# The v rows of an expert layer: every row gathered whole, against half of each row gathered and the other half multiplied from streamed tiles

## The chip, the cores and the metric

One NeuronCore of one Trainium2 chip runs the whole program in one launch. The metric is the device time of an execution in microseconds (us). The core has five engines: TensorE (PE; its weight loads are PEld), VectorE (DVE), ScalarE (ACT), GpSimd (POOL) and SyncE (SP), and 16 DMA engines that all queues share.

## The reference

Two transformer blocks on 256 tokens of width 2048, in fp32. The change touches only the last layer of the second block. For each token, 8 heads choose 16 experts each out of 128 x 128, so 128 experts a token. An expert is a row of `peer_u` and a row of `peer_v`, 2048 floats (8 KB) each.

```python
top_s, top_i = lax.top_k(s, PEER_TOPK)          # per head, two lists of 128 keys
cand_i = (top_i[:, :, 0, :, None] * N_KEYS + top_i[:, :, 1, None, :])...
best_s, best_j = lax.top_k(cand_s, PEER_TOPK)
idx = jnp.take_along_axis(cand_i, best_j, axis=-1)
g = jax.nn.softmax(best_s, axis=-1)
u_sel = jnp.take(u, idx, axis=0)
a = jax.nn.gelu(jnp.einsum('thkd,td->thk', u_sel, hb), approximate=False)
v_sel = jnp.take(v, idx, axis=0)
return jnp.einsum('thk,thkd->td', (g * a).astype(hb.dtype), v_sel)
```

## The kernel before, in words

The 256 tokens are two token tiles of 128, one token to a partition. Everything ahead of the expert layer is a list of products whose weights SyncE streams in tiles of 512 KB; the last of them, `query`, gives the scores. `read_scores(c)` on ScalarE hands the scores of two heads over, and `choose(t, c)` on VectorE turns them into 32 expert numbers a token (t is the token tile, c the pair of heads), so 8 calls in all. The first two calls stand ahead of the first dot product.

The expert layer works in slots. Slot (row) j of token tile t is one gather: an indirect DMA from GpSimd's queue fetches for each of the 128 tokens the row of its j-th expert, 128 rows of 8 KB, 1.05 MB, into one of 16 buffers `rows_buf`. There are 256 such slots for u and 256 for v. The order is by half tile (`hx`, 64 slots): 64 gathers of u, 64 of v, and so on. GpSimd issues in that order, and a gather waits until its pair of buffers has been used (`rows_used`).

- u slots: VectorE multiplies the row by `hb` and adds up (`dot_products`), 2048 columns.
- `coefs(hx)`: gelu of the 64 dots on ScalarE, times the softmax gate, gives a coefficient per token and slot.
- v slots: half of them VectorE adds to `h` with `scalar_tensor_tensor` (`weigh_rows`), the other half TensorE adds up in PSUM: ScalarE makes a diagonal matrix of the coefficients (`diag`), TensorE multiplies it by the row, four products of 512 columns. `add_sums` adds the four banks of a token tile to `h`.
- The calls choose(0, 2) to choose(1, 3) stand between the weighings, two in each of the first three v phases. SyncE writes the output in 8 pieces when the sums are there.

What starts when is set by the order in each engine's own instruction stream and by counting semaphores. An engine that waits holds everything behind it in its stream. For GpSimd that is every later gather.

## Time and profile before

| | |
|---|---|
| Three runs | 3399.82, 3405.42, 3406.12 us; median 3405.42 |
| Profiled execution, span from first to last instruction | 3402.5 us (its time apart from the span is not given) |
| DMA share and rate, 2134 to 3385 us | 1.01, 426 GB/s |
| Data of the indirect gathers (queue q0) | 536.97 MB of 868.10 MB |
| Instructions | 42238 |

The span is cut into stretches by the view of windows, which gives for each the busy time of each engine with its number of instructions, the clock granted to TensorE as a share of the higher level, the busy share of the 16 DMA engines and their GB/s. The expert layer is the stretch from the first dot product at 2134 us to the end. An engine's idle time matters only where the others wait for it.

### The profile page before, as it was taken

Reading aid. Unit: us, or ns where it says so; the run is one execution under the profiler, and the core shown is the slowest. Engines: PE = TensorE matmul, PEld = TensorE weight load, DVE = VectorE, ACT = ScalarE, POOL = GpSimd, SP = SyncE. Lnnn points to the kernel's source line nnn. Section 1 sums busy time; section 2 is a strip of 40 time slices with the busy share of each in tenths; the row PEclk is TensorE's granted clock in tenths of the full one; section 3 lists DMA queues with packets and bytes.
Section 4 is the critical chain, followed back from the end, with each engine's and each line's share of the span. In section 5 each row is a group of like instructions: output and inputs, shape, how many; then the busy total and the mean of one; then the engine's idle time right before and its main releaser. Section 6 shows DMA issues by size and latency. Waiting matters only on the chain.

```text
span 3402.5 us, 42238 instructions
## 1 busy us (share of the span) xinstructions
PE 2507.2 (74%) x15833; PEld 1974.7 (58%) x15833; DVE 1781.8 (52%) x2456; ACT 1081.7 (32%) x2108; POOL 2364.1 (69%) x1677
## 2 busy tenths in 40 slices
PE   7999996989999999989999899108503730571077
PEld 5777885779988998889988679103201310230032
DVE  4375656242200223220412446997797879778954
ACT  6444424464444444454546554000000100000000
POOL 7400316859999999987866579886687578568853
PEclk9999997999999999999999999559856965796589
DMA  5684300546655665555544346999999999999998
GB/s 180 206 237 145 105 3 26 185 123 183 185 191 187 183 183 185 187 153 161 161 131 125 117 164 206 396 427 427 427 428 427 427 427 427 428 426 427 427 427 344
DMA packets 241376, 868.10 MB, mean 255 GB/s; under 512 B 18940, under 2 KB 21484, under 8 KB 174886
## 3 DMA queue, kind: packets, MB, share of 16 engines
q0 software_dynamic: 73776, 536.97, 37.5%
q1 hardware_dynamic: 163414, 316.11, 30.6%
q10 hardware_dynamic: 4016, 12.75, 1.3%
q8 instruction: 106, 1.74, 0.2%
q14 instruction: 64, 0.52, 0.0%
HBM read 860.24 MB, written 2.10 MB: 253 GB/s over the span
## 4 chain that ended last, share of the span: by engine, by line
PE 50%; POOL 19%; DMA 11%; DVE 7%; issue 4%; ACT 1%; DVEq 0%; ACTq 0%; POOLq 0%; SPq 0%
PE acc L2022 20%; PE acc L2032 19%; DMA zone<-in_peer_v,zone 10%; POOL lasting L736 10%; POOL zone L736 9%; PE acc L2028 3%; PE acc L2160 3%; PE acc L2586 2%; POOL w_lo L616 1%; DVE lasting L1962 1%; DMA lasting<-in_peer_u,zone 1%; PE acc L2475 1%; DVE zone L1568 0%; PE acc L2069 0%; DVE x_lo L1697 0%
## 5 line engine op out<-in xcount | busy, mean ns | idle before, releaser
L616 POOL TENSOR_TENSOR w_lo<-lasting,w_hi 128x512 fp32r<-128x512 f32 x1024 | 1372.4, 1359 | 276.0 <-ACT w_hi L785 257.3
L785 ACT ACTIVATE w_hi<-lasting 128x512 fp32r<-128x512 f32 (+1 forms) x1184 | 741.3, 631 | 903.6 <-PE acc L2022 457.0
L2586 PE MATMUL acc<-zone,lasting 128*128 128x512 f32 x512 | 256.3, 655 | 694.3 <-ACT lasting L1297 643.4
L2586 PEld LDWEIGHTS acc<-zone,lasting 128*128 128x128 f32 x512 | 105.2, 210 | 841.6 <-ACT lasting L1297 505.2
L2032 PE MATMUL acc<-x_hi,w_hi 128*128 128x256 f32 (+1 forms) x1856 | 305.5, 286 | 11.5 <-DVE x_lo L1697 4.3
L736 POOL DMA_INDIRECT zone<-in_peer_v,zone x128 | 192.2, 1502 | 165.6 <-DVE lasting L1962 73.6
L1932 DVE CUSTOM_DVE_ANT_0 zone<-zone 128x2048 f32<-128x2048 f32 x128 | 293.4, 2292 | 21.9 <-DMA zone<-in_peer_u,zone 7.1
L1932 DVE CUSTOM_DVE_ANT_0 zone<-lasting,zone 128x2048 f32<-128x2048 f32 x128 | 293.5, 2293 | 21.0 <-DMA lasting<-in_peer_u,zone 8.6
L2032 PE MATMUL acc<-x_lo,w_hi 128*128 128x256 f32 (+1 forms) x1856 | 298.6, 283 | 0.0
L2032 PE MATMUL acc<-x_hi,w_lo 128*128 128x256 f32 (+1 forms) x1856 | 298.3, 283 | 0.0
L2586 PE MATMUL acc<-lasting 128*128 128x512 f32 x512 | 247.8, 635 | 64.9 <-DMA zone<-in_peer_v,zone 38.2
L736 POOL DMA_INDIRECT lasting<-in_peer_u,zone x128 | 248.5, 1942 | 58.4 <-issue 36.9
L736 POOL DMA_INDIRECT zone<-in_peer_u,zone x128 | 256.7, 2005 | 42.7 <-issue 37.8
L2032 PEld LDWEIGHTS acc<-x_hi,w_hi 128*128 128x128 f32 x1856 | 255.0, 189 | 19.1 <-issue 7.7
L2032 PEld LDWEIGHTS acc<-x_lo,w_hi 128*128 128x128 f32 x1856 | 255.3, 189 | 0.0
L2032 PEld LDWEIGHTS acc<-x_hi,w_lo 128*128 128x128 f32 x1856 | 254.4, 189 | 0.0
L736 POOL DMA_INDIRECT lasting<-in_peer_v,zone x128 | 199.5, 1558 | 72.7 <-issue 35.6
L1289 ACT ACTIVATE zone<-zone 128x64 f32<-128x64 f32 x4 | 1.0, 256 | 744.7 <-DVEq L1936 744.7
L2022 PE MATMUL acc<-w_hi,x_hi 128*128 128x512 f32 (+1 forms) x672 | 216.0, 403 | 19.5 <-DVE w_lo L1379 8.8
L2586 PEld LDWEIGHTS acc<-lasting 128*128 128x128 f32 x512 | 101.3, 203 | 209.4 <-issue 196.3
L2022 PE MATMUL acc<-w_hi,x_lo 128*128 128x512 f32 (+1 forms) x672 | 211.1, 396 | 0.0
L2022 PE MATMUL acc<-w_lo,x_hi 128*128 128x512 f32 (+1 forms) x672 | 209.6, 393 | 0.0
(419 smaller groups left out, 3951.7 us busy)
## 6 DMA issues: line engine op xcount, KB each, us to landing
lasting<-in_w_in SPq DMA_DIRECT2D x200, 512.0 KB, 3.7
lasting<-in_w_up SPq DMA_DIRECT2D x128, 512.0 KB, 3.8
lasting<-in_w_down SPq DMA_DIRECT2D x128, 512.0 KB, 3.6
lasting<-in_w_mix_out SPq DMA_DIRECT2D x32, 512.0 KB, 3.6
lasting<-in_w_out SPq DMA_DIRECT2D x32, 512.0 KB, 3.6
lasting<-in_peer_w_query SPq DMA_DIRECT2D x32, 512.0 KB, 3.7
lasting<-in_w_kv_cross SPq DMA_DIRECT2D x16, 512.0 KB, 3.7
lasting<-in_w_q_cross SPq DMA_DIRECT2D x8, 512.0 KB, 3.7
```

What stands on the lines that cost most here:

```text
L616: pool.tensor_tensor(w_lo[:, k, 0:width], ring[:, slot, s % SLOT_SLABS, 0:width], w_hi[:, k, 0:width].bitcast(FP32), ALU.subtract).then_in ...
L736: pool.indirect_dma_start(out=rows_buf[2 * n + k], out_offset=None, in_=A[table][0], in_offset=bass.IndirectOffsetOnAxis(ap=experts[:, hx ...
L785: act.activation(w_hi[:, s % PARTS, 0:width], ring[:, slot, s % SLOT_SLABS, 0:width], ACT.Copy).then_inc(hi_ready, 1)
L1289: act.activation(part, part, ACT.Gelu).then_inc(s_gelu, 1)
L1932: last = dve.tensor_tensor_reduce(out=junk, in0=rows_buf[2 * n + k], in1=hb[:, t], scale=1.0, scalar=0.0, op0=ALU.mult, op1=ALU.add, accum ...
L1962: last = STT(h[:, t], rows_buf[2 * n + k], coef[:, t, slot:slot + 1], h[:, t], ALU.mult, ALU.add)
L2022: last = pe.matmul(bank(banks[t])[:, 0:width], xp[:, s, g.lo + t * P:g.lo + (t + 1) * P], wp[:, k, 0:width], **kw)
L2028: last = pe.matmul(bank(banks[f // 2])[:, f % 2 * SEQ:(f % 2 + 1) * SEQ], wp[:, k, f * P:(f + 1) * P], xp[:, s, g.lo:g.hi], skip_group_che ...
L2032: last = pe.matmul(bank(banks[f])[:, 0:g.hi - g.lo], wp[:, k, f * P:(f + 1) * P], xp[:, s, g.lo:g.hi], **kw)
L2160: return pe.matmul(out, lhsT, rhs, start=start, stop=stop, skip_group_check=check)
L2475: last = pe.matmul(two_out(m), probT2[0:size, m % 2, n * P:(n + 1) * P], v, start=n == 0, stop=n == t + 1)
L2586: last = pe.matmul(bank(4 * t + c), diag[:, n // 2, k], rows_buf[2 * n + k][:, c * CHUNK:(c + 1) * CHUNK], start=hx % 2 == 0 and i == 0 an ...
```

## The change

The v part is split by columns. Columns 1024 to 2047 are still gathered, one slot at a time, as half rows of 4 KB (0.52 MB a gather, `gather_v`). Columns 0 to 1023 are computed without a gather: the coefficients of a token tile are spread into a matrix of 16384 experts by 128 tokens (`dense0`, `dense1`), and the left half of the whole table `peer_v` is streamed by SyncE in tiles of 128 experts by 1024 columns (0.52 MB) and multiplied by it on TensorE (`v_product`).

The matrix is built from one-hot vectors: for each token, TensorE multiplies the one-hots of its 128 slots by the second key with those by the first key, the latter scaled by the coefficients (`dense_group`, four tokens a group, 32 groups a token tile). ScalarE builds the one-hots of the first token tile (`one_hots` by Abs and Relu), VectorE those of the second (by `is_equal`); ScalarE copies the products out of PSUM (`read_dense`).

The order: all 256 u slots first (`gather_u`), with 16 buffers for the first token tile and 7 for the second. From u slot 80 on a v half row follows each u slot until 72 have been sent (`V_AFTER`, `V_EARLY`); TensorE adds these up by diagonals, all of the first token tile. 48 diagonals come ahead of the first matrix, 24 are interleaved with its groups. The other 184 half rows are weighed by VectorE, with 6 buffers. Calls of `choose` come behind u slots 2, 92, 132, 160 and 192, coefficients behind 66, 129, 220 and 255; three calls of choose stand ahead of the first dot. No tile is streamed until all dots are done. Then 11 tiles are multiplied for the first token tile alone while the second matrix is built; these 11 are loaded again for the second token tile, and the other 117 are used for both: 139 loads, 5 places. `choose` also writes the numbers of the half rows and `split_experts` the two keys of each slot.

The core of the diff:

```diff
+        FIRST_TILE, SECOND_TILE = (5, 7, 8, 13, 4, 6, 0, 1, 9, 10, 11, 12, 14, 15), (5, 7, 8, 13, 4, 16, 18)
+        U_BUF = [q if q < 16 else FIRST_TILE[(q - 16) % 14] if q < P else SECOND_TILE[(q - P) % 7] for q in range(U_SLOTS)]
+        U_SEM = [b if b < 16 else b - 7 for b in U_BUF]
+        U_USE = [U_SEM[:q].count(U_SEM[q]) for q in range(U_SLOTS)]
+        U_BEFORE = [max([k for k in range(q) if U_SEM[k] == U_SEM[q]], default=None) for q in range(U_SLOTS)]
+        V_EARLY = 72
+        V_AFTER = {80 + k: k for k in range(V_EARLY)}
+        CHOICES = [(t, c) for t in range(TILES) for c in range(4)]
+        CHOSEN = {choice: n + 1 for n, choice in enumerate(CHOICES)}
+        CHOOSE_AFTER = dict(zip((2, 92, 132, 160, 192), CHOICES[3:]))
+        COEFS_AFTER = {66: 0, 129: 1, 220: 2, 255: 3}
...
+        LATE_HALVES = half_rows + [at(3 * D, HALF_D), at(7 * HALF_D, HALF_D)]
+        half_of_slot = lambda q: half_rows[q % 4] if q < V_EARLY else LATE_HALVES[(q - V_EARLY) % 6]
+        ALONE_BEFORE, ALONE_BESIDE = 0, 11
+        ALONE = ALONE_BEFORE + ALONE_BESIDE
+        V_LOADS = [(i, (0,)) for i in range(ALONE)] + [(i, (1,)) for i in range(ALONE)] + [(i, (0, 1)) for i in range(ALONE, N_KEYS)]
...
+            for n, (i, tiles) in enumerate(V_LOADS):
+                if n == 0:
+                    sp.wait_ge(s_wpe, V_EARLY)
+                if n == ALONE_BEFORE:
+                    sp.wait_ge(s_dot, 2 * TILES)
+                elif n >= ALONE_BEFORE + len(V_SPOTS):
+                    sp.wait_ge(slab_used, v_used(n - len(V_SPOTS)))
+                if n >= 4:
+                    sp.wait_ge(*v_landed(n - 4))
+                sp.dma_start(v_tile(n), A["peer_v_2"][0][i * P:(i + 1) * P, 0:HALF_D]).then_inc(v_landed(n)[0], 16)
...
+            def gather_u(q):
+                t, j, b = q // P, q % P, U_BUF[q]
+                if j % 32 == 0:
+                    pool.wait_ge(s_ix0, CHOSEN[t, j // 32])
+                if U_USE[q]:
+                    pool.wait_ge(s_dotted, U_BEFORE[q] + 1)
+                if b == 16:
+                    pool.wait_ge(s_ix0, CHOSEN[0, 3])
+                elif b == 18:
+                    pool.wait_ge(s_dot, 2)
                 pool.indirect_dma_start(
...
+            def gather_v(q):
+                t, j = q // P, q % P
+                if q >= V_EARLY + 6:
+                    pool.wait_ge(s_wdve, q - 6 - V_EARLY + 1)
+                elif q >= V_EARLY + 4:
+                    pool.wait_ge(s_dot, 2 * TILES)
+                elif q >= V_EARLY:
+                    pool.wait_ge(slab_used, v_used(ALONE_BEFORE - 4 + q - V_EARLY))
+                elif q >= 4:
+                    pool.wait_ge(s_wpe, q - 4 + 1)
+                else:
+                    pool.wait_ge(s_dotted, 4)
+                pool.indirect_dma_start(
+                    out=half_of_slot(q), out_offset=None, in_=v_halves,
+                    in_offset=bass.IndirectOffsetOnAxis(ap=half_rows_no[:, t, j:j + 1], axis=0)
+                ).then_inc(half_landed(q)[0], 16)
...
+            for q in range(7, U_SLOTS):
+                if q == 13:
+                    pool.wait_ge(s_sp, 4)
+                gather_u(q)
+                if q in V_AFTER:
+                    gather_v(V_AFTER[q])
+            for q in range(V_EARLY, U_SLOTS):
+                gather_v(q)
...
+            def diagonal(q):
+                if q >= 4:
+                    act.wait_ge(s_wpe, q - 4 + 1)
+                act.activation(diag[:, q % 4], ident, ACT.Copy, scale=coef[:, 0, q:q + 1]).then_inc(s_diag, 1)
+            def one_hots(g):
+                if g >= 2:
+                    act.wait_ge(s_dense, g - 1)
+                for n in range(4):
+                    s_ = 4 * g + n
+                    for k in range(2):
+                        last = act.activation(hot_of(g, k)[:, n], key_no, ACT.Abs, scale=-1.0, bias=keysT[:, k, s_:s_ + 1])
+                step(last)
+                step(act.activation(one_hot[:, g % 2], one_hot[:, g % 2], ACT.Relu, scale=-1.0, bias=1.0))
+                for n in range(4):
+                    s_ = 4 * g + n
+                    last = act.activation(hot_of(g, 1)[:, n], hot_of(g, 1)[:, n], ACT.Copy, scale=coefT[:, 0, s_:s_ + 1])
+                last.then_inc(s_hot, 1)
+            def read_dense(g):
+                act.wait_ge(s_dense, g + 1)
+                act.activation(dense[g // 32][:, :, 4 * (g % 32):4 * (g % 32) + 4], bank(6 + g % 2).rearrange("p (n c) -> p c n", n=4), ACT.Copy).then_inc(s_denseR, 1)
...
+            gelu_dots(1)
+            exp_gates(2)
+            act.wait_ge(s_coefs, 2)
+            read_keys(0)
+            read_coefs(0)
+            for g in range(GROUPS // TILES):
+                one_hots(g)
+                if g:
+                    read_dense(g - 1)
+                if 48 + g < V_EARLY:
+                    diagonal(48 + g)
+            read_dense(GROUPS // TILES - 1)
+            exp_gates(3)
+            gelu_dots(2)
+            read_keys(1)
+            gelu_dots(3)
+            read_coefs(1)
+            for g in range(GROUPS // TILES, GROUPS):
+                read_dense(g)
...
+            def dot_product(q):
+                t, j, b = q // P, q % P, U_BUF[q]
+                dve.wait_ge(u_full[U_SEM[q]], 16 * (U_USE[q] + 1))
+                dve.tensor_tensor_reduce(out=junk, in0=u_rows[b], in1=hb[:, t], scale=1.0, scalar=0.0,
+                                         op0=ALU.mult, op1=ALU.add, accum_out=dots[:, t, j:j + 1]).then_inc(s_dotted, 1)
+                dve.drain()
...
+            def one_hots(g):
+                dve.wait_ge(s_dense, g - 1)
+                for n in range(4):
+                    s_ = 4 * (g - GROUPS // TILES) + n
+                    TS(hot_of(g, 0)[:, n], key_no, keysT[:, 2, s_:s_ + 1], None, ALU.is_equal)
+                    last = TS(hot_of(g, 1)[:, n], key_no, keysT[:, 3, s_:s_ + 1], coefT[:, 1, s_:s_ + 1], ALU.is_equal, ALU.mult)
+                last.then_inc(s_hot, 1)
+            def weigh_half_row(q):
+                t, j = q // P, q % P
+                dve.wait_ge(*half_landed(q))
+                STT(h[:, t, HALF_D:], half_of_slot(q), coef[:, t, j:j + 1], h[:, t, HALF_D:], ALU.mult, ALU.add).then_inc(s_wdve, 1)
+                dve.drain()
...
+            for t, c in CHOICES[:3]:
+                dve.wait_ge(s_sc, c + 1)
+                choose(t, c)
+            dve.wait_ge(lo_ready, G["query"].slab(0, 3, SLABS - 1) + 1)
+            for q in range(U_SLOTS):
+                dot_product(q)
+                if q % HALF_ROWS == HALF_ROWS - 1:
+                    dve.nop().then_inc(s_dot, 1)
+                if q in CHOOSE_AFTER:
+                    t, c = CHOOSE_AFTER[q]
+                    if t == 0:
+                        dve.wait_ge(s_sc, c + 1)
+                    choose(t, c)
+                    if c == 3:
+                        split_experts(t)
+                if q in COEFS_AFTER:
+                    coefs(COEFS_AFTER[q])
+            dve.wait_ge(s_keysR, 2)
+            dve.wait_ge(s_coefR, 2)
+            done = V_EARLY
+            for g in range(GROUPS // TILES, GROUPS):
+                one_hots(g)
+                if g % 2:
+                    weigh_half_row(done)
+                    done += 1
+            dve.wait_ge(s_wpe, V_EARLY)
             for c in range(2):
+                add_bank(0, 2 + c, 4 + c)
+                dve.drain()
+            for q in range(done, U_SLOTS):
+                weigh_half_row(q)
+            dve.wait_ge(slab_used, v_used(len(V_LOADS) - 1))
+            for t in range(TILES):
+                for c in range(2):
+                    add_bank(t, c, 2 * t + c)
...
+            def weigh_half_row(q):
+                pe.wait_ge(s_diag, q + 1)
+                pe.wait_ge(v_full[q % 4], 16 * (q // 4 + 1))
+                for c in range(2):
+                    last = pe.matmul(bank(4 + c), diag[:, q % 4], half_rows[q % 4][:, c * CHUNK:(c + 1) * CHUNK],
+                                     start=q == 0, stop=q == V_EARLY - 1)
+                last.then_inc(s_wpe, 1)
...
+            def dense_group(g):
+                pe.wait_ge(s_hot, g + 1)
+                if g >= 2:
+                    pe.wait_ge(s_denseR, g - 1)
+                for n in range(4):
+                    last = pe.matmul(bank(6 + g % 2)[:, n * P:(n + 1) * P], hot_of(g, 1)[:, n], hot_of(g, 0)[:, n], start=True, stop=True)
+                last.then_inc(s_dense, 1)
...
+            def v_product(n):
+                i, tiles = V_LOADS[n]
+                pe.wait_ge(*v_landed(n))
+                for t in tiles:
+                    for c in range(2):
+                        last = pe.matmul(bank(2 * t + c), dense[t][:, i], v_tile(n)[:, c * CHUNK:(c + 1) * CHUNK],
+                                         start=i == 0, stop=i == N_KEYS - 1)
+                last.then_inc(slab_used, 1)
...
+            for g in range(GROUPS // TILES):
+                dense_group(g)
+                if 48 + g < V_EARLY:
+                    weigh_half_row(48 + g)
...
+            turn_keys(1)
+            turn_coefs(1)
+            for g in range(GROUPS // TILES, GROUPS):
+                dense_group(g)
+                if g % 3 == 2 and (g - GROUPS // TILES) // 3 < ALONE_BESIDE:
+                    v_product(ALONE_BEFORE + (g - GROUPS // TILES) // 3)
+            pe.wait_ge(s_denseR, GROUPS)
+            for n in range(ALONE, len(V_LOADS)):
+                v_product(n)
```

## Rows read from the trace of the kernel before

**Rows 1.** Windows: busy us (instructions) by engine, granted clock, DMA share, GB/s

```profile
2134.00:3385.00 1251.00, 492.58 (x1029) 205.10 (x1027) 991.46 (x1026) 57.29 (x149) 890.01 (x506) 0.71 1.01 426
...
2900.00:3000.00 100.00, 63.87 (x128) 26.28 (x128) 74.97 (x99) 8.26 (x26) 56.91 (x35) 0.81 1.01 427
3000.00:3100.00 100.00, 61.23 (x128) 25.39 (x128) 73.92 (x96) 5.48 (x11) 65.77 (x44) 0.87 1.01 427
```

**Rows 2.** Groups by line and shape, 2134 to 3402 us: busy us, mean ns, idle before

```profile
L1932 DVE CUSTOM_DVE_ANT_0 zone<-zone 128x2048 f32<-128x2048 f32 x128 | 293.4, 2292 | 21.9 <-DMA zone<-in_peer_u,zone 7.1 <-DMA lasting<-in_peer_u,zone 4.9
L736 POOL DMA_INDIRECT lasting<-in_peer_u,zone x127 | 247.4, 1948 | 58.2 <-issue 36.9 <-PE acc L2586 21.3
L736 POOL DMA_INDIRECT zone<-in_peer_v,zone x128 | 192.2, 1502 | 165.6 <-DVE lasting L1962 73.6 <-PE acc L2586 57.0 <-issue 33.1
L1962 DVE SCALAR_TENSOR_TENSOR lasting<-zone,lasting 128x2048 f32<-128x2048 f32 x64 | 150.5, 2351 | 104.5 <-DMA zone<-in_peer_v,zone 101.4 <-issue 0.4 <-DVE zone L1921 0.2
```

**Rows 3.** Timeline of GpSimd: start us, us, instruction

```profile
2271.35 2.13 POOL L736 DMA_INDIRECT zone<-in_peer_u,zone  x1 [0.30 <-issue]
...
2317.59 0.95 POOL L736 DMA_INDIRECT lasting<-in_peer_v,zone  x1 [0.30 <-issue]
2318.84 0.95 POOL L736 DMA_INDIRECT lasting<-in_peer_v,zone  x1 [0.30 <-issue]
```

**Rows 4.** Timeline of VectorE: two dots, then one call of choose

```profile
2134.32 2.29 DVE L1932 CUSTOM_DVE_ANT_0 zone<-zone 128x2048 f32<-128x2048 f32 x1
...
2146.42 2.29 DVE L1932 CUSTOM_DVE_ANT_0 zone<-lasting,zone 128x2048 f32<-128x2048 f32 x1
...
2326.30 0.30 DVE L1883 MAX8 zone<-zone 128x8 f32<-128x128 f32 x1
...
2339.41 0.19 DVE L1908 TENSOR_TENSOR zone<-zone 128x32 f32<-128x32 f32 x1
...
2344.49 0.19 DVE L1921 SCALAR_TENSOR_TENSOR zone<-zone 128x32 uint32<-128x32 f32 x1
```

**Rows 5.** DMA issues from 2200 to 2260 us: count, median us to landing

```profile
lasting<-in_peer_u,zone POOLq DMA_INDIRECT x14, 9.6
```

**Rows 6.** Windows: weight tiles of 2 KB rows alone, columns as in rows 1

```profile
175.00:176.80 1.80, 1.80 (x10) 1.46 (x9) 0.69 (x1) 0.06 (x1) 0.00 (x0) 1.00 1.03 363
```

**Rows 7.** ScalarE: timeline of two stretches, then groups by line

```profile
2125.22 1.01 ACT L1276 ACTIVATE zone<-acc 128x1024 f32<-128x1024 f32 x1
...
2290.80 2.45 ACT L1297 ACTIVATE lasting<-lasting,zone 128x128 f32<-128x128 f32 x8 [0.84 <-DVEq L1953]
...
L988 ACT ACTIVATE zone<-acc 128x512 f32<-128x512 f32 x18 | 9.8, 594 | 4.2 <-PE acc L2022 4.2
```

**Rows 8.** TensorE: timeline of eight products, and line 2586's ns min/median/max

```profile
3351.50 3.60 PE L2586 MATMUL acc<-zone,lasting 128*128 128x512 f32 x8
...
L2586 PE MATMUL acc<-lasting x512: 592/592/1193, 2303.9 to 3392.0; 128*128 128x512 f32 x171
```

**Rows 9.** VectorE: timeline of two short operations, then groups by line

```profile
2339.52 0.17 DVE L1912 TENSOR_SCALAR zone<-zone 128x32 uint32<-128x32 uint32 x1
2339.60 0.17 DVE L1913 TENSOR_SCALAR zone<-zone 128x32 uint32<-128x32 uint32 x1
...
L1808 DVE TENSOR_SCALAR zone<-acc,lasting 128x128 f32<-128x128 f32 x16 | 5.6, 351 | 0.6
L1477 DVE TENSOR_TENSOR zone<-zone 128x1024 f32<-128x1024 f32 x2 | 2.4, 1218 | 0.0
```

**Rows 10.** The end: windows as in rows 1, then VectorE's timeline

```profile
3380.00:3385.00 5.00, 4.59 (x11) 1.71 (x9) 2.68 (x2) 0.00 (x0) 0.00 (x0) 1.00 0.62 262
3385.00:3390.00 5.00, 2.77 (x4) 1.31 (x5) 2.02 (x1) 0.00 (x0) 0.00 (x0) 0.76 0.06 26
...
3397.05 2.48 DVE L1973 TENSOR_TENSOR lasting<-acc,lasting 128x512 f32<-128x512 f32 x4 [0.26 <-issue]
```

More of the change, by code:

```diff
@@ L131, in build @@
         with nc.sbuf_tensor("lasting", [P, BASE], FP32) as lasting, nc.sbuf_tensor("zone", [P, TOTAL - BASE], FP32) as zone_all:
+            pass
+        with nc.sbuf_tensor("before_dense", [P, X0 + 1024], FP32), nc.sbuf_tensor("dense0", [P, P * N_KEYS], FP32) as dense0, nc.sbuf_tensor("dense1", [P, P * N_KEYS], FP32) as dense1:
             pass
@@ L378, in build @@
+        v_tile = lambda n: half_rows[n % 4] if n < ALONE_BEFORE else at(V_SPOTS[spot_of(n)], HALF_D)
         G = {}
@@ L404, in build @@
         following = dict(zip(list(G)[:-1], list(G)[1:]))
+        TURNS = sum(g.turns * g.bodies for g in G.values())
         tile_full = [sem(f"tile_full{i}") for i in range(SLOTS)]
@@ L741, in _ @@
-            early = [(0, 0), (0, 1), (1, 0), (1, 1), (2, 0)]
-            rests("query", after={at_: lambda n=n, k=k: gather(0, 0, n, k) for at_, (n, k) in zip(((2, 15), (3, 2), (3, 5), (3, 8), (3, 11)), early)})
+            def gather_u(q):
[8 more added lines that the diff above has]
+                    pool.wait_ge(s_dot, 2)
+                pool.indirect_dma_start(
+                    out=u_rows[b], out_offset=None, in_=A["peer_u_2"][0],
+                    in_offset=bass.IndirectOffsetOnAxis(ap=experts[:, t, j:j + 1], axis=0)
+                ).then_inc(u_full[U_SEM[q]], 16)
@@ L1283, in exp_gates, with gelu_dots @@
                 act.activation(part, part, ACT.Exp).then_inc(s_be, 1)
-            exp_gates(0)
-            for hx in range(2 * TILES):
+            def gelu_dots(hx):
                 act.wait_ge(s_dot, hx + 1)
@@ new lines, in _ @@
+            exp_gates(0)
+            gelu_dots(0)
+            exp_gates(1)
+            act.wait_ge(s_coefs, 1)
+            for q in range(48):
+                diagonal(q)
+            gelu_dots(1)
[9 more added lines that the diff above has]
+                    diagonal(48 + g)
@@ L1979, in _ @@
-            for hx in range(2 * TILES):
-                dot_products(hx)
-                coefs(hx)
-                for i in range(ROUNDS):
-                    weigh_rows(hx, i)
-                    if i < 2 and hx + 1 < 2 * TILES:
-                        t, c = (hx + 1) // 2, (hx + 1) % 2 * 2 + i
-                        if t == 0:
-                            dve.wait_ge(s_sc, c + 1)
-                        choose(t, c)
-                    if i == 2 and hx == 2:
-                        add_sums(0)
@@ new lines, in turn_keys @@
+            def turn_keys(t):
+                pe.wait_ge(s_keys, t + 1)
+                if t:
+                    pe.wait_ge(s_denseR, GROUPS // TILES)
+                for k in range(2):
+                    last = pe.transpose(bank(6)[:, k * P:(k + 1) * P], split_keys[:, 2 * t + k], ident)
+                last.then_inc(s_keysT, 1)
+            def v_product(n):
[6 more added lines that the diff above has]
+                last.then_inc(slab_used, 1)
```

218 lines of the change are left out of this document (107 added, 111 removed).

## The prediction

> **What bounds the kernel now.** I read the stretch by stretch busy times first. From 2134 to 3385 us, 1251 of the span's 3402.5 us, the DMA share is 1.01 at 426 GB/s, while GpSimd is busy for 890 us, VectorE for 991 us and TensorE for 493 us [rows 1]. So 512 gathers of 1.05 MB pass one after another at 2.456 us each (1.0486 MB / 427 GB/s), 1257 us, and the end is set by bytes. The reader is to see next how close the others stand. The groups by line give a dot product 2293 ns and a gather 1.9 us while u rows are fetched, 1.5 us while v rows are [rows 2]. GpSimd's timeline says why: a gather takes 0.95 us plus 0.3 us of issue where VectorE pauses and 2.1 plus 0.3 us where it works on 2048 columns [rows 3]. VectorE's dots follow each other every 2.42 us ((2146.42 - 2134.32) / 5) [rows 4]. DMA, VectorE and GpSimd thus need 2.46, 2.42 and 2.42 us for a u row. Fewer bytes in this stage leave two other limits right beside.
>
> **The change in bytes and in engine work.** u stays at 256 gathers of 1.05 MB. v becomes 256 gathers of 0.52 MB and 139 streamed tiles of 0.52 MB: 475.5 MB in place of 536.9. A half-MB transfer moves packets of 4 KB. The bounds of its price: 1.23 us at the 427 GB/s of the 8 KB rows [rows 1], 1.44 us at the 363 GB/s where only 2 KB rows went at a full DMA share [rows 6]. A line through the two packet times (2048 B x 16 / 363 = 90 ns, 8192 B x 16 / 427 = 307 ns) gives 162 ns for 4 KB, 1.30 us; I take 1.28. DMA then needs 256 x 2.456 + 395 x 1.28 = 1134 us, 123 fewer. That is the gain if nothing else interrupts it. Removed are also VectorE's 128 weighings of 2.35 us [rows 2], half of TensorE's 1024 products and 184 of ScalarE's 256 diagonals; none sets the end now, since DMA is full while they run, so they give nothing by themselves.
>
> The Trainium skill, DMA: Bandwidth & Descriptors, Bandwidth, measures 341 GB/s for a transfer of 1 MB and advises 1 MB or more in each. Gathers queued behind each other show 427 GB/s here for 1 MB, so the trace disagrees for this use; as an estimate from that page, a half transfer at 341 GB/s would take 1.54 us and the last stretch below 74 us more.
>
> Now the stretches, each from its own order of waits.
>
> **Start to the dot of row 132.** VectorE makes choose(0, 2) ahead of the first dot and choose(0, 3) behind row 2. Its scores are there (copy at 2125.2 [rows 7]). One choose takes 18.4 us (2326.30 to 2344.68) [rows 4], plus 0.5 for two small operations that the change adds. The first dot moves from 2134.3 to 2154 (18.9, and 0.9 for the additions of the first two), row 3 starts at 2154 + 7.3 + 18.9 + 1.0 (split_experts) = 2181. The 16 first buffers are full by about 2166, so DMA stands for some 20 us, and again partly while GpSimd, in its own order, waits for the dot of row 13 to refill that buffer for u row 19 (2208). From there GpSimd issues one u row per 2.42 us, VectorE takes one per 2.43, and a row lands 9.6 us after its issue [rows 5]: VectorE never waits, and u row 80 is issued at 2208 + 61 x 2.42 = 2356. From there each u row has a half row of v behind it. GpSimd needs 2 x 2.42 = 4.84 us for a pair while VectorE is busy, 2 x 1.25 + 1.17 = 3.67 where VectorE makes one dot in the meantime; DMA needs 2.456 + 1.28 = 3.73. Rows become late from row 82 on; row 92 lands at 2412, and the choose behind it (18.9) is partly used to run ahead. From row 109 on VectorE waits again, and row 132 lands 40 pairs x 3.73 = 149 us after row 92, at 2562. Its dot ends at 2564. Bounds: 2555 (1.23 us, pairs at once) and 2585.
>
> **Row 132 to row 152.** v row 52 waits for TensorE's product of v row 48, that for a diagonal which ScalarE makes behind its first one_hots, and ScalarE first waits for exp_gates(2), which choose(1, 1) releases 13.1 us (2326.30 to 2339.41) behind the dot of row 132. Behind v row 52 stands u row 133 in GpSimd's queue, and for that VectorE waits. From then each pair u, v costs one group of ScalarE: 8 activations 128x128 at 0.306 us (8 in 2.45), one 128x1024 at 1.01, four more at 0.306, the read of 128x512 at 0.59, one diagonal at 0.31 [rows 7]: 2.45 + 1.01 + 1.22 + 0.59 + 0.31 = 5.6, and 0.4 for two chained waits and fills: 6.0 us. Bounds: 5.0 (activations packed closer) to 7.5 (the scattered write of read_dense at twice its price and longer waits). So v 52 goes out at 2564 + 23 (13, then 2 for the transposed columns, 5 for the first group, 3 for diagonal and product), v 71 at +23 + 19 x 6.0 = +137, u row 152 lands at +145, its dot ends at +148. Twenty pairs, 75 us of DMA, take 148.
>
> **Row 153 to row 255.** GpSimd is free, but the second token tile has 7 buffers. 8 dots at 2.45, choose(1, 2) 18.9, 32 dots, choose(1, 3) with its split 19.9, 63 dots at 2.43, coefs 1.2: 20 + 18.9 + 77.8 + 19.9 + 153.1 + 1.2 = 290 us, all VectorE. A buffer's round (2.4 + 9.6 + 2.3) is shorter than 7 x 2.43, so rows don't wait; but 7 buffers hold 17 us of DMA against a choose of 19, and nothing else is queued. u ends at 2564 + 148 + 290 = 3002; coefs, transpose and copy 3 more.
>
> **Second matrix built, 32 groups.** VectorE makes 8 comparisons 128x128 a group. Bounds of one: 0.08 us (two 128x32 start 0.08 apart) and 0.35 (a 128x128 from PSUM) [rows 9]; I take 0.2, near the former's form. Each second group adds a weighing of 1024 columns, 1.22 us [rows 9] plus 0.06. Group: 1.6 + 0.64 = 2.25, in all 73 us (56 to 105). TensorE (4 small products, a third of v_product's 0.9) and ScalarE (0.59) stay below. Meanwhile 16 tiles go (5 at once, 11 as products free them) and 18 halves: 34 x 1.28 = 44 of 76 us. End 3078.
>
> The Trainium skill, SBUF — State Buffer, Who interferes with whom, says that VectorE's tensor_scalar in a two-port mode and a GpSimd operation exclude each other for a whole instruction, which speaks against these comparisons beside gathers. That gathers stretch beside dots, in [rows 3], is contention of this sort; as an estimate by that page, each of 22 gathers could cost VectorE another 0.95 us here, 21 in all. It has no place in the 73.
>
> **The rest.** 162 halves and 123 tiles are left, 285 x 1.28 = 365 us (350 to 410). TensorE needs 117 x 4 x 0.45 + 11 x 2 x 0.45 = 220 us (8 products in 3.60 us [rows 8]), VectorE 168 x 1.28 = 215, GpSimd at most 162 x 2.42 = 392 if every gather met a weighing, but a weighing takes only half of VectorE's time here, so some 300. Both queues are backlogged, tiles end first, about 39 halves go alone; 4 us for that. Last row to the end: weighing 1.3, four sums 2.5 (3397.05 on), output 3.0 (to 3402.5), 1 for waits, 8 in all; now it is 17, since DMA falls off at 3385 [rows 10]. Span: 3078 + 365 + 4 + 8 = 3455, 52.5 us over 3402.5. The profiled execution's times beside its span aren't shown separately; the three runs' median lies 2.9 us above its span, so 3458.
>
> The same sum by DMA's idle time: 2134 to 2564 holds 130.5 u rows and 52 halves, 387 of 430 us; then 148 - 75 = 73; 290 - 258 = 32; 76 - 44 = 32; 4. Idle 184, less 123 of bytes, less 9 at the end: 52 us more.
>
> **Rivals.** *A, bytes decide (faster).* What is queued covers every pause, as it does now over the whole stage [rows 1]. 3402.5 - 123 - 9 = 3270 span, 3273 us. Its place is GpSimd's queue from v row 52 on; it ends ahead of the kernel before from the point where DMA stands for less than 132 us in total. Against it: u row 133 stands behind v row 52 in one queue, and what was issued before is 14 u rows, all needed by the dot of row 132. *B, the clock.* Where TensorE had stood still, a product of 512 columns took up to 1.19 us against 0.59, half the speed [rows 8]; with pauses in the last stretch a tile costs 4 x 0.9 = 3.6 us, 117 x 3.6 + 20 = 441 in place of 365: 3534 us. Against it: TensorE is to be busy 220 of 365 us, and where it was busy 61 and 64 of 100 us the granted clock was 0.87 and 0.81 of the higher level [rows 1], 2.2 us a tile at worst, under the 2.56 that DMA takes for a tile and a half row of v together. *C, small packets.* Half transfers cost what 2 KB rows show, 1.44 us: 285 x 0.16 + 40 x 0.16 = 52 us more, 3510. The page on DMA named above would put it higher still. *D, ScalarE's groups hide* under the 3.73 us of a pair: 19 x 2.27 = 43 less, 3415. For it nothing in the rows; it needs activations of 0.13 us in place of 0.306.
>
> **Numbers.** Chances: forecast 0.70, A 0.11, B 0.05, C 0.07, D 0.07. All lower bounds of the likeliest together (19 for the groups, 17 for the build, 15 for the rest) give 3407, so its own range is 3407 to 3495. The range 3405 to 3510 reaches over D to C, leaving out A, B and the edges of the rest. A difference within 0.2% (7 us) can't be told from no change. Faster 0.12 (A and a little), same 0.06, slower 0.82.
>
> **What would show it.** First dot near 2154; u row 132's dot near 2564, then a pause of GpSimd of some 20 us or more; 20 gathers of each kind at 6 us a pair; DMA share near 0.5 there, near 0.85 to u's end at 3002; a matrix of 73 us; then 365 us at a share of 1. The forecast is wrong if ScalarE's group differs by over 2 us, if the half transfers run slower than 1.4 us, or if the pause at row 132 is covered.

## The result, and the profile after

The changed kernel takes 3522.7 us, median of 4 runs (3518.8 to 3529.6), against 3403.8 us for the kernel before (4 runs): ratio 1.0352, interval [1.0337, 1.0367]. It is slower, by 119 us where 53 were forecast, and the time lies outside the range of 3405 to 3510. The profiled execution has a span of 3519.0 us, 116.5 more.

One execution of E3 below took 5795 us, and its ratio is formed without it.

The forecast gave times for the ends of its stretches. VectorE's timeline of the changed kernel shows the dots of slots 0, 132, 133, 152 and 255 (start us, us, instruction; in brackets the idle time before and its releaser):

```profile
2152.67 2.29 DVE L2078 CUSTOM_DVE_ANT_0 zone<-zone 128x2048 f32<-128x2048 f32 x1
...
2567.72 2.29 DVE L2078 CUSTOM_DVE_ANT_0 zone<-zone 128x2048 f32<-128x2048 f32 x1 [1.33 <-DMA zone<-in_peer_u,lasting]
...
2603.29 2.29 DVE L2078 CUSTOM_DVE_ANT_0 zone<-zone 128x2048 f32<-128x2048 f32 x1 [14.48 <-DMA zone<-in_peer_u,lasting]
...
2707.35 2.29 DVE L2078 CUSTOM_DVE_ANT_0 zone<-zone 128x2048 f32<-128x2048 f32 x1 [2.91 <-DMA zone<-in_peer_u,lasting]
...
2998.26 2.29 DVE L2078 CUSTOM_DVE_ANT_0 zone<-lasting,zone 128x2048 f32<-128x2048 f32 x1
```

The first dot was forecast at 2154, the end of slot 132's at 2564 (it is 2570), of slot 152's at 2712 (2709.6), of the last at 3002 (3000.6). Up to there the kernel is the one that was forecast, within 6 us at each of these places. The second matrix takes 10 us longer, and the last stretch 58. For the last stretch, TensorE's timeline, and its line in the page's groups:

```profile
3098.99 1.98 PE L2779 MATMUL acc<-lasting,dense 128*128 128x512 f32 x4 [1.56 <-DMA lasting<-in_peer_v]
...
3111.64 401.97 PE L2779 MATMUL acc<-lasting,dense 128*128 128x512 f32 x936 [0.54 <-DMA lasting<-in_peer_v]
...
L2779 PE MATMUL acc<-lasting,dense 128*128 128x512 f32 x1024 | 447.2, 597 | 5.0 <-DMA lasting<-in_peer_v 4.3
```

The count matters here. `v_product` issues 22 x 2 + 117 x 4 = 512 products, and the trace has 1024 records: an fp32 product is two of them. The 117 shared tiles are 936 records without a pause in 402 us, 3.44 us a tile. The same stood in the trace of before. Its 128 rows on TensorE are 4 products each, 512 in all. [rows 8] show 512 records on one line; the other line of the same view has 512 more, so 1024 in all:

```profile
L2586 PE MATMUL acc<-zone,lasting x512: 592/592/1222, 2291.7 to 3395.4; 128*128 128x512 f32 x171
```

The 8 records of 3.60 us in [rows 8] are therefore four products of one row, not eight.

The windows (columns as in [rows 1]) show where DMA has pauses:

```profile
2154.00:2200.00 46.00, 0.00 (x0) 0.00 (x0) 42.61 (x89) 0.00 (x0) 8.07 (x3) 0.50 0.27 104
...
2600.00:2700.00 100.00, 63.83 (x221) 36.59 (x222) 41.44 (x36) 98.85 (x274) 45.02 (x36) 0.88 0.81 287
...
2800.00:2900.00 100.00, 0.66 (x2) 0.29 (x2) 93.63 (x133) 2.18 (x4) 69.52 (x33) 0.50 0.84 344
2900.00:3000.00 100.00, 0.00 (x0) 0.00 (x0) 94.09 (x85) 0.00 (x0) 82.83 (x40) 0.50 0.99 414
...
3001.00:3087.00 86.00, 59.84 (x302) 41.35 (x303) 81.08 (x277) 19.38 (x33) 16.87 (x18) 0.91 0.60 197
...
3200.00:3300.00 100.00, 100.00 (x234) 44.32 (x233) 64.94 (x51) 0.00 (x0) 51.80 (x51) 1.00 1.03 419
3400.00:3500.00 100.00, 100.00 (x234) 44.33 (x233) 16.70 (x13) 0.00 (x0) 7.94 (x8) 1.00 0.64 216
```

From 2570 to 2710 us, where half rows wait for ScalarE, the share is 0.67 (near 0.5 was forecast), from there to the end of the u rows 0.90 (0.85). From 3200 us DMA is full at 419 GB/s, a half-MB transfer in 1.25 us (0.524 MB / 419 GB/s; 1.28 was taken). The half rows end near 3425, and from then on VectorE stands until TensorE has finished. VectorE's timeline at the end, last weighing and first of the four sums:

```profile
3423.75 1.28 DVE L2111 SCALAR_TENSOR_TENSOR lasting<-zone,lasting 128x1024 f32<-128x1024 f32 x1 [1.16 <-DMA zone<-in_peer_v,lasting]
3513.64 2.48 DVE L2116 TENSOR_TENSOR lasting<-acc,lasting 128x512 f32<-128x512 f32 x4 [88.61 <-PE acc L2779]
```

### The profile page after: what moved, and what is told of

It reads as the page before. It is cut to its first block, busy times and chain, and to the rows that moved or that the text cites. A ratio compares the mean times of both kernels' runs of the same rounds, so it can differ in the third digit from the quotient of the medians.

```text
span 3519.0 us, 45043 instructions
## 1 busy us (share of the span) xinstructions
PE 2698.3 (77%) x16639; PEld 2093.9 (60%) x16639; DVE 1781.9 (51%) x2790; ACT 1247.6 (35%) x2534; POOL 2247.3 (64%) x1677
## 4 chain that ended last, share of the span: by engine, by line
PE 59%; DVE 16%; POOL 8%; ACT 4%; issue 3%; DMA 2%; DVEq 0%; ACTq 0%; POOLq 0%; SPq 0%
PE acc L2183 19%; PE acc L2193 17%; PE acc L2779 12%; DVE zone L2078 7%; POOL lasting L808 3%; PE acc L2189 3%; POOL zone L828 3%; PE acc L2321 2%; POOL zone L808 2%; ACT lasting L1393 1%; DVE lasting L2104 1%; PE acc L2636 1%; DMA zone<-in_peer_v,lasting 1%; ACT lasting L1398 1%; DMA zone<-in_peer_u,lasting 1%
## 5 line engine op out<-in xcount | busy, mean ns | idle before, releaser
L2779 PE MATMUL acc<-lasting,dense 128*128 128x512 f32 x1024 | 447.2, 597 | 5.0 <-DMA lasting<-in_peer_v 4.3
L828 POOL DMA_INDIRECT zone<-in_peer_v,lasting x196 | 258.8, 1320 | 260.7 <-DVE lasting L2111 145.3
L2744 PE MATMUL acc<-zone,lasting 128*128 128x512 f32 x288 | 159.9, 684 | 310.2 <-DMA zone<-in_peer_v,lasting 310.2
L2779 PEld LDWEIGHTS acc<-lasting,dense 128*128 128x128 f32 x1024 | 195.0, 192 | 247.9 <-issue 237.7
L808 POOL DMA_INDIRECT lasting<-in_peer_u,lasting x128 | 229.0, 1789 | 106.1 <-DVE zone L2078 68.3
L2744 PEld LDWEIGHTS acc<-zone,lasting 128*128 128x128 f32 x288 | 56.7, 219 | 395.9 <-issue 391.8
L808 POOL DMA_INDIRECT zone<-in_peer_u,lasting x128 | 232.1, 1813 | 66.4 <-issue 37.5
L2183 PE MATMUL acc<-w_hi,hid_lo 128*128 128x512 f32 x640 | 199.6, 401 | 0.0
L2111 DVE SCALAR_TENSOR_TENSOR lasting<-zone,lasting 128x1024 f32<-128x1024 f32 x124 | 159.2, 1284 | 78.8 <-DMA zone<-in_peer_v,lasting 78.1
```

Of the source, the lines that this page charges most:

```text
L808: pool.indirect_dma_start(out=u_rows[b], out_offset=None, in_=A["peer_u_2"][0], in_offset=bass.IndirectOffsetOnAxis(ap=experts[:, t, j:j + ...
L828: pool.indirect_dma_start(out=half_of_slot(q), out_offset=None, in_=v_halves, in_offset=bass.IndirectOffsetOnAxis(ap=half_rows_no[:, t, j: ...
L2111: STT(h[:, t, HALF_D:], half_of_slot(q), coef[:, t, j:j + 1], h[:, t, HALF_D:], ALU.mult, ALU.add).then_inc(s_wdve, 1)
L2183: last = pe.matmul(bank(banks[t])[:, 0:width], xp[:, s, g.lo + t * P:g.lo + (t + 1) * P], wp[:, k, 0:width], **kw)
L2744: last = pe.matmul(bank(4 + c), diag[:, q % 4], half_rows[q % 4][:, c * CHUNK:(c + 1) * CHUNK], start=q == 0, stop=q == V_EARLY - 1)
L2779: last = pe.matmul(bank(2 * t + c), dense[t][:, i], v_tile(n)[:, c * CHUNK:(c + 1) * CHUNK], start=i == 0, stop=i == N_KEYS - 1)
```

## The experiments

There are ten kernels, and all ratios are to the kernel before. "Less" and "more" compare with the changed kernel's 3522.7 us where no other is named. Places in a span (the dot of slot 255, for instance) are from one profiled execution of each kernel. The part ahead of the expert layer, which no experiment changes, ends some us earlier or later in each of these executions, so such places are compared with that in mind.

**E1: half of TensorE's work in the last stretch.** For 116 of the shared tiles the products of the second token tile are left out; the output is incomplete there.

```diff
-                for t in tiles:
+                for t in (tiles if len(tiles) == 1 or i == N_KEYS - 1 else tiles[:1]):
```

> The changed kernel, with the products of the second token tile left out for 116 of the 117 shared tiles (its left half of the sums is therefore incomplete); every transfer and every wait stays. Theory (TensorE sets the last stretch: a product of 512 columns is recorded as two passes of 0.427 us, 0.855 us together, 3.42 us a shared tile): 116 x 1.71 = 198 us less work on TensorE, 220 left, so DMA takes over with some 285 x 1.25 = 356 us; from 3087 on 360 to 370 us in place of 427, a time of 3455 to 3470. Rival (the stream is held by its five places and its landing time, not by the work of TensorE): within 10 us of 3522.

Measured: 3476.8 us, ratio 1.0212 [1.0188, 1.0236], 46 us under the changed kernel and 7 over the forecast band. One window of its last stretch:

```profile
3100.00:3200.00 100.00, 79.14 (x161) 27.07 (x159) 50.92 (x41) 0.00 (x0) 39.00 (x41) 1.00 1.02 414
```

TensorE now has pauses, DMA is full, and the transfers and waits are unchanged. So TensorE's work set the last stretch, and the half rows and tiles come some 46 us below it. The 7 us over the band lie at the end. TensorE has its last tile at 3415, and the half rows that are left go alone, with six buffers:

```profile
3415.00:3467.00 52.00, 0.26 (x1) 0.00 (x0) 46.09 (x37) 0.00 (x0) 35.77 (x32) 0.53 0.91 334
```

VectorE's weighings follow each other every 1.44 us there (six in 8.66 us), where DMA at its full rate has a half row every 1.25; over these 52 us that makes about 7.

**E2: 24 streamed tiles beside the u slots.**

```diff
-        ALONE_BEFORE, ALONE_BESIDE = 0, 11
+        ALONE_BEFORE, ALONE_BESIDE = 24, 11
```

> The changed kernel with 24 tiles for the first token tile alone streamed and multiplied beside the u slots (24 more loads in all, 163). Theory (TensorE sets the last stretch): 24 x 1.71 = 41 us of its work move from there to a stretch where it is idle, and 24 x 1.25 = 30 us of transfers go beside u slots 170 to 255, where VectorE sets the pace and DMA has some 30 us free. 3480 to 3500. Rival (bytes set the end): 30 us more, 3550.

Measured: 3526.0 us, ratio 1.0364 [1.0347, 1.0382]. Neither: no gain, no 30 us of loss. The dot of slot 255 starts at 3019.5, 21 us later than in the changed kernel; from there to the end it takes 504 us in place of 521. So beside the u slots there was less room than I reckoned, and of TensorE's 41 us only 17 came off at the end. E7 shows where the other 24 went.

**E7: as E2, with the second token tile's own loads between shared ones.**

```diff
-        V_LOADS = [(i, (0,)) for i in range(ALONE)] + [(i, (1,)) for i in range(ALONE)] + [(i, (0, 1)) for i in range(ALONE, N_KEYS)]
+        V_LOADS = [(i, (0,)) for i in range(ALONE)]
+        for i in range(ALONE):
+            V_LOADS += [(i, (1,)), (ALONE + i, (0, 1))]
+        V_LOADS += [(i, (0, 1)) for i in range(2 * ALONE, N_KEYS)]
```

> As the kernel with 24 tiles beside the u slots (3526 us), with the 35 loads for the second token tile alone alternating with shared ones. Theory (those 35 came one after another at DMA's 2.5 us each where TensorE needs 1.71, so TensorE stood for some 20 us and the gain was lost): 3503 to 3512. Rival (the gain was lost in the u slots only, 20 us later there): 3520 to 3530.

Measured: 3495.4 us, ratio 1.0281 [1.0260, 1.0302], 31 us under E2 with the same end of the u slots (3020). The window behind the second matrix, first of E2:

```profile
3100.00:3200.00 100.00, 79.13 (x180) 31.23 (x181) 58.73 (x68) 2.39 (x4) 39.36 (x40) 0.97 0.95 375
```

and of E7:

```profile
3100.00:3200.00 100.00, 96.61 (x246) 44.50 (x245) 58.63 (x65) 2.39 (x4) 39.63 (x40) 1.00 0.97 383
```

The granted clock and DMA are nearly the same, and TensorE has 66 records more. Its timeline behind the second matrix says why, first E2:

```profile
3195.69 1.98 PE L2779 MATMUL acc<-lasting,dense 128*128 128x512 f32 x4 [0.52 <-DMA lasting<-in_peer_v]
3198.20 319.57 PE L2779 MATMUL acc<-lasting,dense 128*128 128x512 f32 x744 [0.53 <-DMA lasting<-in_peer_v]
```

and E7:

```profile
3108.94 379.65 PE L2782 MATMUL acc<-lasting,dense 128*128 128x512 f32 x884 [0.69 <-ACT dense L1406]
```

A tile with two products (four records, 1.72 us of work) comes every 2.5 us in E2, and TensorE waits for 31 of them, one after another. In E7 they alternate with tiles of four products, and TensorE doesn't wait again until its last product. That is 31 x 0.8 = 25 us where the expectation reckoned some 20; 4 us more lie ahead, since TensorE begins this stretch at 3108.9 and in E2 at 3112.6. Together they are the 29 us between the two profiled executions.

**E3: 48 early half rows.** `V_EARLY = 72` becomes 48. No half row is then tied to ScalarE's groups.

```diff
-        V_EARLY = 72
+        V_EARLY = 48
```

> The changed kernel with 48 early half rows in place of 72: none is then tied to ScalarE's groups, and the 24 others are weighed by VectorE at the end. Theory (GpSimd's queue is held by ScalarE at slots 132 to 152): from the dot of slot 132 to that of 152 it takes 19 + 20 x 2.43 = 68 us in place of 140; the 24 halves more in the last stretch lie under TensorE's 427 us there (309 x 1.25 = 386 us of DMA). 3445 to 3460. Rival (the seven buffers of the second token tile set that pace): 3505 to 3525.

Measured: 3443.8 us, ratio 1.0110 [1.0087, 1.0132], 79 us less. From the dot of slot 132 (2565.1) to that of slot 152 (2632.4) it takes 67 us where 68 were expected and the changed kernel has 140. The stretch behind the second matrix stays TensorE's, although DMA has 24 transfers more.

**E10: the same 72 half rows, 24 of them sent later.** Only GpSimd's order changes.

```diff
-        V_AFTER = {80 + k: k for k in range(V_EARLY)}
+        V_AFTER = {80 + k if k < 48 else 136 + 5 * (k - 48) // 2: k for k in range(V_EARLY)}
```

> The changed kernel with all 72 early half rows, of which the last 24 are issued behind every second or third u slot from 136 on (every 5 slots two), in place of behind slots 128 to 151. ScalarE's groups, diagonals and products are unchanged. Theory (at slot 132 GpSimd's queue waits for choose(1, 1) and then for one group of ScalarE a pair): the u rows run on, the dot of slot 152 comes some 50 us earlier; the 24 half rows cost up to 1.25 us each further on. 3465 to 3485. Rival (ScalarE's groups hold the u rows in another way, say by the buffers that TensorE reads): 3505 to 3525.

Measured: 3470.5 us, ratio 1.0207 [1.0192, 1.0223], 52 us less. ScalarE's and TensorE's instructions are as in the changed kernel, so what held the u rows was their place in GpSimd's queue behind half rows that wait for ScalarE.

**E4: two calls of choose later.**

```diff
-        CHOOSE_AFTER = dict(zip((2, 92, 132, 160, 192), CHOICES[3:]))
+        CHOOSE_AFTER = dict(zip((30, 60, 92, 132, 160, 192), CHOICES[2:]))
...
-            for t, c in CHOICES[:3]:
+            for t, c in CHOICES[:2]:
```

> The changed kernel with choose(0, 2) behind slot 30 and choose(0, 3) behind slot 60, in place of ahead of the first dot and behind slot 2. Theory (DMA stands at the start since all 16 buffers are full and VectorE is choosing): DMA runs on through both calls, the dot of slot 132 ends near 2530 in place of 2570, a time of 3477 to 3492. Rival (VectorE's own work is the limit up to slot 132, wherever the calls stand): 3515 to 3525.

Measured: 3508.1 us, ratio 1.0303 [1.0283, 1.0323], 15 us less and not the 30 to 45 of the theory. Slot 67 starts at 2336.4 against 2336.7: VectorE has the same 67 dots and two calls of choose behind it in both, and never waited. So DMA's pause at the start (share 0.27 from 2154 to 2200) cost nothing up to there. But GpSimd stands 18 us further ahead when the half rows begin; u row 80 and v row 0, first in the changed kernel, then in E4:

```profile
2354.75 2.13 POOL L808 DMA_INDIRECT lasting<-in_peer_u,lasting  x1 [0.30 <-issue]
2357.18 2.13 POOL L828 DMA_INDIRECT zone<-in_peer_v,lasting  x1 [0.30 <-issue]
...
2336.24 0.94 POOL L808 DMA_INDIRECT lasting<-in_peer_u,lasting  x1 [0.30 <-issue]
2337.49 1.98 POOL L828 DMA_INDIRECT zone<-in_peer_v,lasting  x1 [0.30 <-issue]
```

The gain appears between slot 82 (2372.9 against 2373.8) and slot 92 (2403.2 against 2414.0) and is 12 us at slot 132 (2556.0 against 2567.7).

**E5: 24 early half rows.** `V_EARLY = 24`, and the first loops over diagonals end there.

```diff
-        V_EARLY = 72
+        V_EARLY = 24
...
-            for q in range(48):
+            for q in range(min(48, V_EARLY)):
```

> The changed kernel with 24 early half rows, in place of 72 (or 48, which took 3444 us). Theory (each half row sent among the u slots costs VectorE about 1.25 us of waiting, since GpSimd issues one gather per 2.42 us while VectorE works; in the last stretch it is free as long as TensorE's 427 us are above DMA's): u ends 24 x 1.25 = 30 us earlier than with 48, the rest keeps 427 us over (309 + 24) x 1.25 = 416. 3405 to 3425. Rival (the u slots are set by VectorE's own work from slot 80 on, or the rest is already set by DMA): 3440 to 3450.

Measured: 3416.7 us, ratio 1.0048 [1.0032, 1.0065], 27 us under E3 where 30 were reckoned. The dot of slot 255 starts at 2881.7 (E3: 2923.1). Of these 41 us, 10 lie ahead of the expert layer, where ScalarE's last copy of scores starts at 2127.9 (E3: 2137.9), and 31 are the u rows'. The rest takes 6 us longer than in E3, 525 and 520 us.

**E8: no weighing between VectorE's one-hots.**

```diff
                 one_hots(g)
-                if g % 2:
-                    weigh_half_row(done)
-                    done += 1
```

> The changed kernel without the 16 weighings between VectorE's one-hots; they follow later. Theory (VectorE sets the 86 us of the second matrix, a comparison costs 0.28 or 0.34 us; the rest is set by TensorE, whose 427 us stay over 301 x 1.25 = 376 of DMA): 16 x 1.28 = 20 us less, 3498 to 3506. Rival (TensorE's or ScalarE's part of a group sets the matrix, or the halves moved to the end set it): within 8 us of 3522.

Measured: 3497.9 us, ratio 1.0283 [1.0265, 1.0300], 25 us less. From the last dot's end to TensorE's first product behind the matrix it takes 68.4 us (2995.4 to 3063.8) and in the changed kernel 86.3, 18 us less where 20 were reckoned; another 5 us lie ahead of the last dot, where the edit changes nothing. VectorE sets the second matrix.

**E6: combined.** E4's and E5's edits, E7's order of loads, and 16 tiles beside the second matrix, one behind every second group:

```diff
-        ALONE_BEFORE, ALONE_BESIDE = 0, 11
+        ALONE_BEFORE, ALONE_BESIDE = 0, 16
...
-                if g % 3 == 2 and (g - GROUPS // TILES) // 3 < ALONE_BESIDE:
-                    v_product(ALONE_BEFORE + (g - GROUPS // TILES) // 3)
+                if g % 2 == 1 and (g - GROUPS // TILES) // 2 < ALONE_BESIDE:
+                    v_product(ALONE_BEFORE + (g - GROUPS // TILES) // 2)
```

> 24 early half rows, choose(0, 2) and choose(0, 3) behind slots 30 and 60, 16 tiles in place of 11 multiplied beside the second matrix, and the loads for the second token tile alone alternate with shared ones. From 3414: some 5 to 12 us less by the calls of choose, 5 x 1.71 = 9 by the tiles, up to 9 by the alternation. 3384 to 3400 by the theory that TensorE's 418 us and DMA's 416 set the last stretch together; 3405 to 3420 by the rival that one of them holds the other through the five places of the stream.

Measured: 3407.2 us, ratio 1.0010 [1.0000, 1.0020]; 10 us under E5, above the 3384 to 3400 of the theory and within the rival's 3405 to 3420. The two profiled executions differ ahead of the expert layer, which has to be taken out first. ScalarE's last copy of scores, E5, then E6:

```profile
2127.91 1.02 ACT L1366 ACTIVATE zone<-acc 128x1024 f32<-128x1024 f32 x1 [2.21 <-PE acc L2727]
...
2139.32 1.02 ACT L1369 ACTIVATE zone<-acc 128x1024 f32<-128x1024 f32 x1 [2.20 <-PE acc L2730]
```

E6 is 11 us behind here and level at slot 120 (2493.6, in E5 2493.2). It catches up between slot 67 and slot 92, in 66 us against 77, where E4 did. From the dot of slot 255 to the end both take 525 to 526 us. So the calls of choose gave about 11 us, and the tiles and the alternation nothing. At the end TensorE is done before VectorE is. Timeline of TensorE, then of VectorE:

```profile
3369.63 10.89 PE L2782 MATMUL acc<-lasting,dense 128*128 128x512 f32 x25
...
3394.99 5.42 DVE L2114 SCALAR_TENSOR_TENSOR lasting<-zone,lasting 128x1024 f32<-128x1024 f32 x4 [1.11 <-DMA zone<-in_peer_v,lasting]
3400.50 2.48 DVE L2119 TENSOR_TENSOR lasting<-acc,lasting 128x512 f32<-128x512 f32 x4
```

TensorE ends at 3380.5, the last half row is weighed at 3400.4: with 24 early half rows the transfers set the last stretch, at a DMA share of 1.03 from 3000 to 3350 us, and TensorE's savings don't show. E9 bears this out: it takes twelve transfers out of this stretch, and the stretch gets 20 us shorter. That the five places of the stream hold anything, as the rival has it, isn't shown.

**E9: twelve half rows in the pause of a choose.** On E6: after u slot 215, when VectorE begins choose(1, 3), 12 half rows go out at once; their diagonals and products stand behind the first matrix's groups.

```diff
-        V_EARLY = 24
-        V_AFTER = {80 + k: k for k in range(V_EARLY)}
+        V_EARLY = 36
+        V_AFTER = {80 + k: [k] for k in range(24)} | {215: range(24, V_EARLY)}
...
-        CHOOSE_AFTER = dict(zip((30, 60, 92, 132, 160, 192), CHOICES[2:]))
+        CHOOSE_AFTER = dict(zip((30, 60, 92, 132, 160, 208), CHOICES[2:]))
...
-                    pool.wait_ge(slab_used, v_used(ALONE_BEFORE - 4 + q - V_EARLY))
+                    pool.wait_ge(s_wpe, V_EARLY)
```

> The combined kernel (3407 us) with 36 early half rows: 24 as there, 12 more issued in one go behind u slot 215, which is when VectorE begins choose(1, 3), now behind slot 208. Theory (with 7 buffers DMA and GpSimd stand in each call of choose, and the last stretch of the combined kernel is set by DMA since TensorE ends some 15 us ahead of the last weighing): 12 x 1.25 = 15 us of transfers move into a pause, 3390 to 3400, faster than both kernels. Rival (the u rows behind them come late by as much as they take): 3402 to 3412.

Measured: 3394.7 us, ratio 0.9973 [0.9964, 0.9982]: faster than both kernels, by 0.3% and 3.6%. The profiled executions show a loss and a gain. VectorE waits for u row 216, which stands in GpSimd's queue behind the twelve:

```profile
2790.45 2.29 DVE L2081 CUSTOM_DVE_ANT_0 zone<-zone 128x2048 f32<-128x2048 f32 x1 [8.23 <-DMA zone<-in_peer_u,lasting]
```

That is 8 us lost. From the dot of slot 255 to the end it takes 506 us in place of E6's 526, 20 won. The difference of 12 is that of the medians. TensorE and VectorE now end together; VectorE's last weighings and sums:

```profile
3380.43 5.42 DVE L2114 SCALAR_TENSOR_TENSOR lasting<-zone,lasting 128x1024 f32<-128x1024 f32 x4
3385.94 2.49 DVE L2119 TENSOR_TENSOR lasting<-acc,lasting 128x512 f32<-128x512 f32 x4
```

## Why the prediction was wrong, point by point

**The sum by stretches**, forecast and profile: start to the dot of slot 132, end at 2564 and 2570 (+6); to slot 152, 148 and 139.6 us (-8); to slot 255, 290 and 291 (+1); coefficients and second matrix, 76 and 86.3, from 3000.6 to TensorE's first shared or second-tile product at 3086.9 (+10); from there to the last product, 369 and 426.7 (+58); the end, 8 and 5.4 (-3). Together 64, the difference between 3455 and 3519. The forecast is so close at 3087 us (9 us) partly by luck, since a group of ScalarE was priced too high and one of VectorE too low.

**The step that failed** is TensorE's term in "The rest": "TensorE needs 117 x 4 x 0.45 + 11 x 2 x 0.45 = 220 us (8 products in 3.60 us [rows 8])". The 0.45 us is one of two records of a product. The 490 products are 980 records at 0.427 us (100 us / 234 in the window from 3200), 419 us. With 220 DMA's 365 ruled; with 419 TensorE does. That the larger of the two sets the stretch was right; TensorE's term had half its size. With 419 in the place of 365 and the 4 for half rows alone, the sum gives 3505 and not 3455. E1 shows it from the other side: with its work halved the kernel gets 46 us faster and DMA fills up. The check was at hand in the 1024 records of before.

The same count is wrong where the prediction lists what is removed, "half of TensorE's 1024 products". The kernel before issues 512 products of 512 columns, the changed one 144 for the early half rows and 512 for the tiles: 656, and 256 smaller ones for the two matrices. TensorE's work grows. Nor has the kernel before 256 diagonals: its trace has 128, and that of the changed kernel 72. None of the signs that the prediction names for being wrong came (a group 2 us off, half transfers over 1.4 us each, no pause at row 132). They leave TensorE out, since at 220 of 365 us it seemed far from mattering.

**Rival B** named the right engine for the wrong reason. It doubled the price by the clock, and the granted clock was 1.00 from 3200 us on. Its 441 us for the stretch lie near the 427 measured, since a record at half the clock (up to 1.19 us, [rows 8]) costs what two at full clock do (0.59 us each there). That isn't evidence for it.

**Row 132 to 152** was right in its mechanism, and E3 and E10 confirm it. GpSimd's timeline, v row 51, u row 132, then v row 52 and u row 133:

```profile
2556.57 0.95 POOL L828 DMA_INDIRECT zone<-in_peer_v,lasting  x1 [0.30 <-issue]
2557.82 2.01 POOL L808 DMA_INDIRECT zone<-in_peer_u,lasting  x1 [0.30 <-issue]
2594.13 0.95 POOL L828 DMA_INDIRECT zone<-in_peer_v,lasting  x1 [34.29 <-PE acc L2744]
2595.38 0.94 POOL L808 DMA_INDIRECT zone<-in_peer_u,lasting  x1 [0.30 <-issue]
```

It waits 34 us, and v row 52 goes out 24 us behind the dot of slot 132 (forecast 23). ScalarE's timeline shows a group:

```profile
2589.36 2.43 ACT L1393 ACTIVATE lasting<-lasting 128x128 f32<-128x128 f32 x8
2591.82 1.06 ACT L1395 ACTIVATE lasting<-lasting 128x1024 f32<-128x1024 f32 x1
2592.91 1.28 ACT L1398 ACTIVATE lasting<-lasting 128x128 f32<-128x128 f32 x4
2594.10 0.57 ACT L1403 ACTIVATE dense<-acc 128x512 f32<-128x512 f32 x1
2594.57 0.39 ACT L1384 ACTIVATE lasting<-lasting 128x128 f32<-128x128 f32 x1
```

From 2589.36 to the next group at 2594.86 are 5.5 us; 6.0 were taken, 0.4 of it for waits that hardly show. 19 x 0.5 = 9.5 us, which is the -8.

**The second matrix** was mis-sized, mostly by the comparisons. Groups by line from 3001 to 3087 us:

```profile
L2104 DVE TENSOR_SCALAR lasting<-lasting 128x128 f32<-128x128 f32 x128 | 45.3, 355 | 0.0
...
L2103 DVE TENSOR_SCALAR lasting<-lasting 128x128 f32<-128x128 f32 x128 | 36.3, 284 | 4.6 <-PE acc L2761 2.2 <-ACT lasting L1407 1.0
L828 POOL DMA_INDIRECT zone<-in_peer_v,lasting x12 | 11.3, 944 | 53.4 <-DVE lasting L2111 48.0 <-issue 5.5
```

A comparison is recorded at 0.28 or 0.36 us on average, but neighbours overlap. What counts is from start to start, in VectorE's timeline of two groups:

```profile
3052.88 0.27 DVE L2103 TENSOR_SCALAR lasting<-lasting 128x128 f32<-128x128 f32 x1
3053.08 0.33 DVE L2104 TENSOR_SCALAR lasting<-lasting 128x128 f32<-128x128 f32 x1
3053.33 1.27 DVE L2111 SCALAR_TENSOR_TENSOR lasting<-zone,lasting 128x1024 f32<-128x1024 f32 x1
3054.70 0.29 DVE L2103 TENSOR_SCALAR lasting<-lasting 128x128 f32<-128x128 f32 x1
...
3058.36 1.27 DVE L2111 SCALAR_TENSOR_TENSOR lasting<-lasting 128x1024 f32<-128x1024 f32 x1
```

Two groups take 5.03 us (3053.33 to 3058.36) where 4.5 were reckoned: 1.37 for the weighing, and 3.66 for 16 comparisons, 0.23 each where 0.2 was taken. Over 32 groups that is 8 us. Another 3 are the last group's products and copy, from 3084.1 to 3086.9, which the sum left out; the wait before the first group was 1 us shorter. 86 us lie within the bounds of 56 to 105. E8 shows VectorE as its limit.

**Start to slot 132** was right in its times and half right in its reasons. DMA stands at the start, and VectorE doesn't wait for it there; what the pause costs comes later, since GpSimd has less of a lead when the half rows begin. E4 won back 12 us of the forecast's 43 us of DMA's idle time. Such an account adds up to the right total, and doesn't say how much of a pause an edit can win back.

**Rivals A, C and D** are out: from 2154 to 3513 us DMA moved 462 MB, 1082 of 1359 us at 427 GB/s, so it stood for 277 us and not under 132; a half transfer cost 1.25 us and not 1.44, and a group took 5.5 us and not 3.7.

**The pages.** 341 GB/s for 1 MB, by the Trainium skill, DMA: Bandwidth & Descriptors, Bandwidth, isn't what queued transfers show: 419 GB/s here with transfers of half a MB. The estimate of 21 us, worked out from the Trainium skill, SBUF — State Buffer, Who interferes with whom, is not borne out. Gathers between VectorE's comparisons took 0.944 us each, as where VectorE pauses in [rows 3]. The comparisons beside one lose little: two of them start 0.45 us apart as a rule (3052.43 to 3052.88) and at most 0.48 beside the gather at 3049.85, so the 18 gathers cost VectorE under 1 us in all, by an estimate from these times. Why gathers take 2.1 us beside the dots of 2048 columns, no run here shows.

What stays open is how much of DMA's other idle time a different order could win back.
